# Retention heads on one Trainium2 core: values and outputs laid out by tokens, two weight units sharing both banks for the values, value products one unit sooner

## The reference

```python
q = rope(q); k = rope(k) * 128 ** -0.5            # 512 x 128
scores = (q @ k.T) * decay                        # causal; in the reference in chunks of 128 tokens and a state
o = scores @ v                                    # 512 x 256
o = (o - mean(o)) * rsqrt(mean((o - mean(o)) ** 2) + 1e-6) * gn_w      # over the 256 values of one token
y_b += (o * silu(g)) @ w_ret_branch[head]
```

## Time and profile before

| what | us |
|---|---|
| median of 3 runs (lowest, highest) | 2577.57 (2577.47, 2578.15) |
| the profiled execution's own time | 2577.84 |
| its span in the profile | 2576.1 |
| TensorE busy | 2558.5 (99% of the span) |
| GpSimd busy | 1514.9 (59%) |
| VectorE busy | 1486.3 (58%) |
| ScalarE busy | 838.6 (33%) |

### The profile page before, as it was taken

The page is one execution under the profiler, slowest core; times in us unless marked ns, Lnnn a source line. Parts: engine busy times, 40 slices in busy tenths (PEclk is TensorE's granted clock), DMA queues, the critical chain, the costliest instruction groups (busy, mean ns, idle before and its releaser), DMA issues.

```text
span 2576.1 us, 32876 instructions
## 1 busy us (share of the span) xinstructions
PE 2558.5 (99%) x11723; PEld 2062.5 (80%) x11723; DVE 1486.3 (58%) x2084; ACT 838.6 (33%) x1157; POOL 1514.9 (59%) x1820
## 2 busy tenths in 40 slices
PE   8999999999999999999999999999999999999999
PEld 7767778888888887778888888888778888888887
DVE  7756774487474737845583442754773448344275
ACT  5444442233222343354321111134334432111112
POOL 7634446666666755555565655765554556565576
PEclk9999999999999999999999999999999999999999
DMA  5311113222222332222322222233222222222223
GB/s 208 115 66 50 55 61 131 98 83 98 99 97 98 109 111 82 83 82 82 106 99 98 98 97 92 89 114 105 77 85 84 82 106 98 99 98 97 92 89 130
DMA packets 36829, 247.44 MB, mean 96 GB/s; under 512 B 4464, under 2 KB 4848, under 8 KB 7792
## 3 DMA queue, kind: packets, MB, share of 16 engines
q1 hardware_dynamic: 34704, 238.57, 26.2%
q10 hardware_dynamic: 2016, 7.35, 0.8%
HBM read 243.81 MB, written 2.10 MB: 95 GB/s over the span
## 4 chain that ended last, share of the span: by engine, by line
PE 31%; POOL 30%; issue 22%; DVE 0%; POOLq 0%; DMA 0%; ACT 0%; DVEq 0%; SPq 0%; ACTq 0%
POOL w_lo L377 30%; PE bank L832 7%; PE bank L834 7%; PE bank L833 7%; PE both L833 3%; PE both L834 3%; PE both L832 3%; PE bank L1281 0%; PE both L1257 0%; PE bank L1243 0%; PE bank L1241 0%; PE bank L1242 0%; DMA raw<-stream 0%; POOLq L415 0%; POOLq L374 0%
## 5 line engine op out<-in xcount | busy, mean ns | idle before, releaser
L377 POOL TENSOR_TENSOR w_lo<-raw,w_hi 128x256 fp32r<-128x256 f32 x1784 | 1492.6, 868 | 964.2 <-ACT w_hi L434 963.2
L434 ACT ACTIVATE w_hi<-raw 128x1024 fp32r<-128x1024 f32 x446 | 469.1, 1056 | 981.6 <-PE bank L834 476.8
L832 PE MATMUL bank<-a_hi,w_hi 128*128 128x512 f32 x1440 | 582.1, 404 | 0.0
L834 PE MATMUL bank<-a_hi,w_lo 128*128 128x512 f32 x1440 | 562.3, 390 | 0.0
L833 PE MATMUL bank<-a_lo,w_hi 128*128 128x512 f32 x1440 | 561.3, 390 | 0.0
L832 PEld LDWEIGHTS bank<-a_hi,w_hi 128*128 128x128 f32 x1440 | 270.5, 188 | 63.7 <-issue 10.3
L834 PEld LDWEIGHTS bank<-a_hi,w_lo 128*128 128x128 f32 x1440 | 270.3, 188 | 58.3
L833 PEld LDWEIGHTS bank<-a_lo,w_hi 128*128 128x128 f32 x1440 | 270.9, 188 | 54.7 <-issue 3.1
L832 PE MATMUL bank<-y_hi,w_hi 128*128 128x512 f32 x696 | 272.4, 391 | 0.0
L834 PE MATMUL bank<-y_hi,w_lo 128*128 128x512 f32 x696 | 270.9, 389 | 0.0
L833 PE MATMUL bank<-y_lo,w_hi 128*128 128x512 f32 x696 | 270.8, 389 | 0.0
(11 more groups left out here) (343 smaller groups left out, 3279.6 us busy)
## 6 DMA issues: line engine op xcount, KB each, us to landing
raw<-stream SPq DMA_DIRECT2D x223, 1024.0 KB, 4.8
h<-xT SPq DMA_DIRECT2D x8, 256.0 KB, 5.9
h<-xT ACTq DMA_DIRECT2D x1, 2048.0 KB, 8.1
outT<-h SPq DMA_DIRECT2D x8, 256.0 KB, 2.3
h<-decay ACTq DMA_DIRECT2D x1, 1024.0 KB, 4.8
h<-rope ACTq DMA_DIRECT2D x1, 1024.0 KB, 9.3
prob<-pT ACTq DMA_DIRECT2D x2, 512.0 KB, 4.4
par<-par ACTq DMA_DIRECT2D x2, 408.0 KB, 3.3
```

The costliest lines, as they stand in the source:

```text
L377: pool.tensor_tensor(w_lo[:, s, part], raw[:, s, part], w_hi[:, s, part], ALU.subtract).then_inc(lo_done, 1)
L434: act.activation(w_hi[:, s, cols], raw[:, s, cols], ACT.Copy).then_inc(hi_done, 1)
L832: pe.matmul(dst, w_hi[:, s, cols], rhs_hi(k), start=start and k == 0, stop=False)
L834: ins = pe.matmul(dst, w_lo[:, s, cols], rhs_hi(k), start=False, stop=stop and k == nk - 1)
```

## The change

It lays the values and outputs of a retention head out by tokens. The two value units are packed by input tiles 0 to 3 and 4 to 7, each with all 256 value columns, and `value_unit` takes the activations as the stationary operand and 256 weight columns as the moving one, with the results of all four token tiles in both banks, over both units; VectorE takes the banks out straight to `rv` with the factor by token (`token_root`, computed once in head 0). The score blocks use `b_r0` and `b_r1` in two pairs; `ret_values` runs in unit 5, with tokens on the partitions. Mean and squares are accumulated by ScalarE along the free axis: four copies with a sum in unit 5, four `Square` with a sum in unit 7, ahead of `Silu` and of the copy of step 7. The two matmuls with the matrix of ones go. VectorE normalises in slot 0 of the next head, TensorE turns the outputs back (`turn_outputs`) in unit 1 of the next head, for the last head between the units 1 and 2 of `U_YA`, and VectorE multiplies by the gate in slot 1. VectorE takes out unit 1 ahead of the probabilities of step 2, and unit 2 behind those of step 3. GpSimd has no retention work any more.

```diff
+out_rows = [(rq, rk)[i // 2][:, i % 2 * RDV:(i % 2 + 1) * RDV] for i in range(QT)]
...
-    def gate_output(t):
...
-    def scale_output(t):
...
     for t in range(RH):
         for j in range(3, RET_UNITS + 3):
-            if j == 7 and t > 0:
-                scale_output(t - 1)
-            if j == 10:
-                gate_output(t)
             lo_part(t * RET_UNITS + U_RET + j, j % 4)
-    scale_output(RH - 1)
...
-            if j == 4:
-                rps.up(3)
-                value_rows(0, b_r0)
             if j == 5:
-                rps.up(3)
-                value_rows(1, b_r1)
-            if j == 6:
-                rps.up(2)
+                rps.up(6)
                 act.wait_ge(product_ready, rps.now())
-                act.activation(rq, b_r0[:, :], ACT.Copy).then_inc(outputs_copied, 1)
-                act.activation(rk, b_r1[:, :], ACT.Copy).then_inc(outputs_copied, 1)
-                rps.up(1)
-                if t > 0:
-                    output_hi(t - 1)
+                for i, rows in enumerate(out_rows):
+                    ins = act.activation(rows, (b_r0, b_r1)[i // 2][:, i % 2 * RDV:(i % 2 + 1) * RDV],
+                                         ACT.Copy, accum_out=out_mean[:, i:i + 1])
+                ins.then_inc(outputs_copied, 1)
+            if j == 6 and t > 0:
+                output_hi(t - 1)
             if j == 7 and t < RH - 1:
                 turn_query(t + 1)
             if j == 7:
-
+                act.wait_ge(output_mean_ready, t + 1)
+                for i, rows in enumerate(out_rows):
+                    ins = act.activation((ssum[:, :], tile_c)[i // 2][:, i % 2 * RDV:(i % 2 + 1) * RDV], rows, ACT.Square,
+                                         bias=out_mean[:, i:i + 1], accum_out=out_root[:, i:i + 1])
+                ins.then_inc(output_squares_done, 1)
                 act.wait_ge(evac, u0 + 11)
                 act.activation(rg, rg, ACT.Silu).then_inc(activated, res.up())
             copy_transposed([(pt[:, :, 0:n], scores[:, :, 0:n])])
             if j == 7:
-                tile_root(ssum[:, :], b_r1[:, :], 1.0 / RDV)
+                load_table(ACT.Sqrt)
+                act.wait_ge(output_squares_done, t + 1)
+                act.activation(out_root, out_root, ACT.Sqrt, bias=eps, scale=1.0 / RDV)\
+                    .then_inc(root_ready, root.up())
                 load_table(ACT.Exp if t < RH - 1 else ACT.Sigmoid)
...
+        def ret_values(i):
+            dst = (b_r0, b_r1)[i // 2][:, i % 2 * RDV:(i % 2 + 1) * RDV]
+            for a in range(i + 1):
+                at = sum(S - c * P for c in range(a)) + (i - a) * P
+                ins = pe.matmul(dst, rp[:, at:at + P], rv[:, a, :], start=a == 0, stop=a == i,
+                                skip_group_check=True)
+            if i % 2 == 1:
+                ins.then_inc(product_ready, rps.up())
+
+        def turn_outputs(t):
+
+            pe.wait_ge(output_normed, t + 1)
+            for e in range(2):
+                for i in range(QT):
+                    ins = pe.transpose((b_r0, b_r1)[e][:, i * P:(i + 1) * P],
+                                       out_rows[i][:, e * P:(e + 1) * P], ident)
+            ins.then_inc(output_turned, 1)
...
             if j == 3:
-                pe.wait_ge(product_read, rfree.due())
-                ret_transposes(b_r0, tile_c)
-                pe.wait_ge(product_read, rfree.due())
-                ret_scores(2, b_r1)
+                pe.wait_ge(product_read, rfree.due(2))
+                ret_scores(2, b_r0)
+                ret_scores(3, b_r1)
             if j == 4:
-                pe.wait_ge(value_rows_copied, 2 * t + 1)
-                ret_scores(3, b_r0)
-                pe.wait_ge(product_read, rfree.due())
-                ret_transposes(b_r1, tile_b)
-            if j == 5:
-                pe.wait_ge(product_read, rfree.due())
-                pe.wait_ge(value_rows_copied, 2 * t + 2)
-                ret_values(0, b_r0)
-                ret_values(1, b_r1)
-            if j == 6:
-                pe.wait_ge(outputs_copied, 2 * t + 2)
-                pe.wait_ge(retention_input_ready, rin.due())
-                pe.matmul(b_r0[:, :], ones, tile_c, start=True, stop=True)\
-                    .then_inc(product_ready, rps.up())
+                pe.wait_ge(product_read, rfree.due(2))
+                pe.wait_ge(evac, u0 + 8)
+                for i in range(QT):
+                    ret_values(i)
 
...
+            if k == 3 and j == 1 and t > 0:
+                turn_outputs(t - 1)
...
+        def value_unit(j):
+            s, cols = conv_unit_slot(j)
+            pe.wait_ge(lo_done, (u0 + j + 1) * LO_PARTS)
+            for i in range(QT):
+                if j == 2 and i % 2 == 0:
+                    pe.wait_ge(evac, u0 + i // 2 + 5)
+                dst = bank[i // 2][:, i % 2 * RDV:(i % 2 + 1) * RDV]
+                rows = slice(i * P, (i + 1) * P)
+                for o in range(4):
+                    k = 4 * (j - 2) + o
+                    if o % 2 == 0:
+                        beside(j, 2 * i + o // 2)
+                    w = slice(cols.start + o * RDV, cols.start + (o + 1) * RDV)
+                    pe.matmul(dst, a_hi[:, k, rows], w_hi[:, s, w], start=k == 0 and i % 2 == 0, stop=False,
+                              skip_group_check=True)
+                    pe.matmul(dst, a_hi[:, k, rows], w_lo[:, s, w], start=False, stop=False,
+                              skip_group_check=True)
+                    ins = pe.matmul(dst, a_lo[:, k, rows], w_hi[:, s, w], start=False,
+                                    stop=k == KD - 1, skip_group_check=True)
+                if (j, i) == (3, 1):
+                    ins.then_inc(value_half_done, 1)
+            ins.then_inc(unit_done, 1)
...
+            elif j in (2, 3):
+                value_unit(j)
...
-            if j == 7:
-                square_sum()
...
+    turn_outputs(RH - 1)
     for j in range(2, YA_UNITS):
...
-            dst = tile_c if j == 2 else tile_b
-            scaled(dst, src, u0, j)
-            V.tensor_copy(small[:, 20:21], dst[:, 0:1])\
-                .then_inc(retention_input_ready, rin.up())
-            V.wait_ge(retention_input_ready, rin.now())
+            if j == 2:
+                V.wait_ge(value_half_done, t + 1)
+            else:
+                arrive(u0, j)
+            tokens = slice(2 * j - 4, 2 * j - 2)
+            leave(u0, j, V.tensor_tensor(rv[:, tokens, :], src.rearrange("p (a f) -> p a f", f=RDV),
+                                         token_root[:, tokens].unsqueeze(2).to_broadcast([P, 2, RDV]),
+                                         ALU.mult))
...
-    def inverse_root(t, quarter):
...
+    def output_norm(t):
+        V.wait_ge(root_ready, root.due())
+        V.reciprocal(out_root, out_root).then_inc(vector_step, steps.up())
+        V.wait_ge(vector_step, steps.now())
+        for i, rows in enumerate(out_rows):
+            ins = V.tensor_scalar(rows, rows, out_mean[:, i:i + 1], out_root[:, i:i + 1],
+                                  ALU.add, ALU.mult)
+        ins.then_inc(output_normed, 1)
+    def output_gate(t):
+        V.wait_ge(activated, res.due())
+        V.wait_ge(output_turned, t + 1)
+        for e in range(2):
+            V.tensor_tensor(rg[:, e, :], (b_r0, b_r1)[e][:, :], rg[:, e, :], ALU.mult)\
+                .then_inc(output_gated, 1)
...
+    def output_mean(t):
+        V.wait_ge(outputs_copied, t + 1)
         rps.due(2)
-        V.tensor_tensor(tile_c, rq, rk, ALU.add).then_inc(retention_input_ready, rin.up())
-        V.wait_ge(retention_input_ready, rin.now())
+        V.tensor_scalar(out_mean, out_mean, -1.0 / RDV, None, ALU.mult).then_inc(output_mean_ready, 1)
...
         if j == 2:
             if last is not None:
-                V.wait_ge(output_gated, 4 * last + 4)
+                V.wait_ge(output_gated, 2 * last + 2)
             rope_sum(rq).then_inc(vector_step, steps.up())
+            scaled(tile_a, bank[1][:, :], t * RET_UNITS + U_RET, 1)
         if j == 7 and t < RH - 1:
             next_query(t + 1)
-        if j > 0 and j not in (2, 6):
+        if j > 0 and j not in (2, 3, 6):
             unit_in(t, j - 1)
         elif j == 0 and last is not None:
             unit_in(last, 7)
...
         step_probs(t, j)
         if j == 2:
-            unit_in(t, 1)
+            V.sem_inc(wait_placed, 1)
+            V.stream_shuffle(tile_b, tile_a, SWAP_RET).then_inc(vector_step, steps.up())
+        if j == 3:
+            unit_in(t, 2)
...
+            V.wait_ge(compressed_values_ready, 1)
+            V.tensor_tensor(tile_a.rearrange("p (i f) -> p i f", f=P),
+                            rstd[:, :].rearrange("p (i f) -> p i f", f=P),
+                            ident.unsqueeze(1).to_broadcast([P, QT, P]), ALU.mult)\
+                .then_inc(vector_step, steps.up())
+            V.wait_ge(vector_step, steps.now())
```

(54 more changed lines are left out.)

44 lines of the change are left out of this document (6 added, 38 removed).

## The result

The changed kernel takes 2595.55 us (median of 4 runs, 2595.41 to 2595.84), the kernel before 2577.86 on the same chip (4 runs): ratio 1.0069, 95% interval [1.0056, 1.0082]. It is 17.7 us slower. The forecast was 2588.5, its own range 2583 to 2593, the whole range 2580 to 2597; the clock rival's 2596 is where the time lies.

The account below looks back on a forecast made before the run. The prediction took TensorE's single file of matmuls, busy 99%, as the bound. Terms 2.6 + 5.5 + 2.9 + 0.4 - 0.5 = +10.9 on the profiled 2577.84 gave 2588.7, median 2588.5 us; own range 2583 to 2593, whole range 2580 to 2597.

Parts of the forecast that it names:

- the clock rival: TensorE's clock falls in the new gaps, each costing about 2 us more, 6 to 8 in all: 2596; chance 0.10.
- ScalarE in unit 7: Four squares ahead of step 7's copy delay TensorE's values: +2.0, +1.6, +1.6, +0.3 us by head, +5.5 in all.
- End of the stage: Unit 2 of `U_YA` waits for the last head's turned and gated outputs: 3.8 us later, 0.9 of it moved transposes: +2.9.
- Value units: 48 matmuls of 256 columns at 0.120 us replace 24 of 512 at 0.226: +0.33 a unit, +2.6 in eight.
- VectorE's slots: Unit 2's second token pair wants unit 1's bank earlier: +0.4 us; the longest wait for `prob` in head 0 shrinks: -0.5.
- matmuls 0.226 apart right behind the gaps: Sign of being right: TensorE's matmuls keep their full-rate spacing of 0.226 us after the new idle times.
- signs of being wrong: `pt` waits under 1 us; 0.45 spacings behind a gap; over 0.13 between value matmuls; `evac` waits in every head's unit 2.
- Loads that don't overlap: Loads for fp32r value matmuls don't overlap, spacing 0.176 us: +3.0 a value unit, 24 in eight: 2610; chance 0.05.
- VectorE 1 us late in each head: GpSimd's traffic slows norm and gate, so slots 1 to 3 start late, 1 us a head: 2592.5; chance 0.08.
- Not slower: The squares don't hold step 7's copy in unit 7: 2577.8; chance 0.13, of it 0.05 with a real gain.

Follow-up runs that it names:

- sq6: Changed kernel with the four squares moved behind ScalarE's copy of step 6 and the mean's small operation one VectorE slot earlier: 2581.14 us.
- narrow_to_wide: Changed kernel with squares behind step 6's copy and merge-gate units before the output's gate, plus 24 value matmuls of 512 columns for 48 of 256: 2575.67 us.
- ahead7_swap: Changed kernel with squares behind step 6's copy, merge-gate units first, weight rounding moved from unit 7, Silu behind step 7's copy, step 7's transposes three matmuls later: 2571.53 us.
- ya: Changed kernel with VectorE taking out units 0 and 1 of the merge gate before it gates the turned outputs: 2589.97 us.
- sq_split: Changed kernel with two of the four squares moved behind the copy of step 6 and two left in unit 7: 2588.23 us.
- before_sq4: Kernel before with four unread ScalarE squares added in unit 7 of each head, ahead of the copy of step 7: 2585.33 us.
- fill: Changed kernel with 46 idle matmuls, results never read, put into TensorE's gaps behind unit 7 of heads 0 to 2 and the last turned outputs: 2589.35 us.

## Why the prediction was right and wrong

**Direction and mechanism: right, for 9.4 of the 17.9 us.** A file of matmuls with thin covers, ScalarE's list of unit 7 as the largest term, the end of the stage as the second. Each stood where it was put, and the rows of before were enough to find them.

**ScalarE in unit 7, +5.5: right as a wait.** Squares were (242.44 - 240.95) / 3 = 0.50 apart, 0.50 was taken. The Trainium skill's (ScalarE: Activation LUTs, What ACT_TABLE_LOAD costs) estimate of 0.40 was set against the row's 0.47, and the trace sides with the row: each square is followed by a read of the accumulator of its own, of 0.19 us. sq6 returns 7.9 us of waiting for moving them, more than 5.5, since in the changed kernel TensorE comes earlier to the gap than before: it has lost mean and square sum. The term compared the same point before and after and had that in it.

**End of the stage, +2.9: right.** TensorE waited 3.07 us in unit 2 of `U_YA`, and that place moved by 3.72 against 3.8 in the working, transposes included.

**Value units, +2.6: a term that was mis-sized.** The 0.120 came out. The other side of the difference, 0.226, came from units of another stage; in the unit itself it is 0.231, which leaves 1.7 of the 2.6. The term also left out that TensorE waits for VectorE's probabilities in unit 2 with matmuls of either size. By narrow_to_wide it is about 1.0.

**VectorE's slots, +0.4 and -0.5.** Of the -0.5, 0.2 came: the longest wait for `prob` in head 0 fell from 0.69 to 0.47 us; the other one there fell too, but it varies between 0.3 and 0.6 in the traces of either layout. The +0.4 shows in no wait of its own. Three new waits of 0.55 stand in unit 7 of heads 1 to 3 and bring the total from 1.3 to 2.5, since the transposes of step 7 at the old place come 0.6 us early once the mean's matmuls ahead of them are gone. The prediction had seen that these transposes can't start earlier; in the changed kernel the wait costs nothing more, as TensorE waits for the copy of the same unit anyway. ahead7_swap removed it.

**The clock: the step that failed.** The prediction held "matmuls 0.226 apart right behind the gaps", and gave the clock rival 0.10 with 6 to 8 us. It is 8.5 by the windows, 6.2 by the medians with fillers, which keep one fall elsewhere. What is left of the growth of the span without it is 9.4, against the forecast's 10.9. Of its own signs of being wrong one came true: 0.42 between the matmuls behind a gap. The argument against it, "the only row is of a far longer gap", was no evidence: a row of a longer gap gives no lower bound for a shorter one. And the prediction put the gap into its own forecast ("TensorE will then stand still for about 3 us") without asking the price of that state. The Trainium skill (TensorE: Matmul & The Clock Gate, What's actually happening) had said that idleness lowers the clock; the trace agrees, with 0.57 and 0.79 behind gaps of 3.0 to 3.5 us. So 2595.55 lies above the forecast's own range (2583 to 2593). That it lies inside the whole range, 2580 to 2597, is owed to the rival with a chance of 0.10 that the range was stretched to take in. And that the rival's 2596 is so near is in part luck: the clock cost more than its 6 to 8 us, and the other terms 1.5 less than their sum.

**The other rivals.** Loads that don't overlap: out, by 0.120. VectorE 1 us late in each head: out, no such wait is in the trace. Not slower: out, since the squares do hold the copy (sq6); but the gain in matmuls that it counted on is real. The file became shorter by 1.9 us a head, and once the two orders were mended and ScalarE's list of unit 7 was shortened, that showed as 6.3 us.

## What to carry to other kernels

Where TensorE is 99% busy, a new gap costs more than its length: price the matmuls behind it at the lower clock, here 1.7 us for each gap of 3 us and 3.4 for one of 3.5. Before work is put onto an idle-looking engine, write down that engine's list between the two points at which the full one meets it, and place the work in the unit where the list has room; four squares cost 14.4 us in unit 7 and nothing to be seen in unit 6, where ScalarE stands idle for 1.64 us even with them. And when a change that removes matmuls comes out slower, give the old kernel the same reordering as the new one before dropping it.

## What was not expected of the hardware

Gaps much shorter than the one at the start bring the lower clock. In the profiled executions it fell with each of the ten idle times of 2.5 us and more behind the start: 3.51, 3.07, 3.03 and 3.03 (changed kernel), 3.51, 3.02 and 3.02 (ya), 3.07 (sq6), 3.07 and 2.53 (sq_split). It also fell with 2.09 (before_sq4) and 1.9 (fill), and not with 0.91 to 1.65, nor with 2.04 twice (sq_split). Around 2 us the length alone doesn't decide; what does wasn't tested.

Fillers whose results nobody reads are a cure as well as a probe: 46 matmuls made the kernel 6.2 us faster.
